# A fused block kernel on one core: the self attention's scores from one f32 matmul each to three matmuls in the rounded f32 form

## The reference, cut to what matters

```python
q = rms_norm(q, q_norm)          # (1, 1024, 8, 96), then rotary on the last 32
k = rms_norm(k, k_norm)
...
s = jnp.einsum('bqhd,bkhd->bhqk', qblk, k).astype(jnp.float32) * scale
p = jax.nn.softmax(s, axis=-1).astype(v.dtype)
return jnp.einsum('bhqk,bkhd->bqhd', p, v)
```

## Time and profile before

| | |
|---|---|
| median of 3 runs | 3533.15 us (3527.78 to 3535.71) |
| the profiled execution | 3533.38 us, span 3531.6 us, mean granted clock 0.944 |
| PE / PEld / DVE / ACT / POOL busy | 3136.1 / 2289.8 / 1394.0 / 905.2 / 149.6 us |
| `head_pairs` in the trace | 574.4 (first scores) to 826.8 us (last result stored) |

### The profile page before, as it was taken

The page is one execution under the profiler, slowest core; times in us unless marked ns, Lnnn a source line. Parts: engine busy times, 40 slices in busy tenths (PEclk is TensorE's granted clock), DMA queues, the critical chain, the costliest instruction groups (busy, mean ns, idle before and its releaser), DMA issues. The chain is left out here.

```text
span 3531.6 us, 35284 instructions
## 1 busy us (share of the span) xinstructions
PE 3136.1 (89%) x14324; PEld 2289.8 (65%) x14324; DVE 1394.0 (39%) x2157; ACT 905.2 (26%) x1452; POOL 149.6 (4%) x226
## 2 busy tenths in 40 slices
PE   7997777998898876887884998999999899999997
PEld 7786744446676663332332887888777688888886
DVE  3126846884444334111115647521215323333334
ACT  3432334443334210000004130021321232222221
POOL 0001011000000001111112000000000000000000
PEclk9998989999999997998996999999999899999999
DMA  3111000003220046999994131111112111111111
GB/s 96 48 46 4 10 13 1 1 1 113 72 84 7 30 194 244 420 421 419 413 399 196 36 75 64 51 48 48 33 57 96 36 48 48 48 48 50 52 48 72
DMA packets 140066, 370.01 MB, mean 105 GB/s; under 512 B 45888, under 2 KB 59840, under 8 KB 113920
## 3 DMA queue, kind: packets, MB, share of 16 engines
q1 hardware_dynamic: 129552, 346.97, 27.3%
q0 software_dynamic: 9216, 16.80, 1.3%
q10 hardware_dynamic: 1152, 4.19, 0.3%
HBM read 352.70 MB, written 32.83 MB: 109 GB/s over the span
## 5 line engine op out<-in xcount | busy, mean ns | idle before, releaser
L2546 PE MATMUL moe_ph<-moe_wgu,moe_rowsT 128*64 128x512 f32 x1024 | 265.4, 678 | 66.8 <-DMA moe_wgu<-in_moe_w_up_dram 37.7
L582 PE MATMUL mlp_ps<-mlp_high,mlp_w_cut 128*128 128x512 f32 x1024 | 317.3, 391 | 2.6 <-PEq L274 2.6
L582 PE MATMUL mlp_ps<-mlp_w_cut,mlp_hidden_high 128*128 128x512 f32 x1024 | 315.2, 389 | 0.0
L482 DVE TENSOR_TENSOR m_w_cut<-m_w_raw,m_w_cut 128x512 fp32r<-128x512 f32 (+1 forms) x86 | 80.8, 940 | 430.7 <-ACT m_w_cut L478 430.4
L482 DVE TENSOR_TENSOR mlp_w_cut<-mlp_w_raw,mlp_w_cut 128x1024 fp32r<-128x1024 f32 x63 | 77.2, 1225 | 397.0 <-ACT mlp_w_cut L478 396.6
L2546 PEld LDWEIGHTS moe_ph<-moe_wgu,moe_rowsT 128*64 128x64 f32 x1024 | 85.2, 155 | 226.7 <-issue 201.4
L582 PEld LDWEIGHTS mlp_ps<-mlp_high,mlp_w_cut 128*128 128x128 f32 x1024 | 193.5, 189 | 43.3 <-issue 3.0
L582 PEld LDWEIGHTS mlp_ps<-mlp_w_cut,mlp_hidden_high 128*128 128x128 f32 x1024 | 192.2, 188 | 39.9
L478 ACT ACTIVATE m_w_cut<-m_w_raw 128x512 fp32r<-128x512 f32 (+1 forms) x86 | 71.4, 831 | 515.3 <-PE m_gates_ps L582 192.8
L478 ACT ACTIVATE mlp_w_cut<-mlp_w_raw 128x1024 fp32r<-128x1024 f32 x63 | 66.7, 1058 | 526.1 <-PE mlp_ps L582 524.5
L582 PE MATMUL mlp_ps<-mlp_low,mlp_w_cut 128*128 128x512 f32 x512 | 200.1, 391 | 0.0
(11 more groups left out here) (534 smaller groups left out, 5850.4 us busy)
## 6 DMA issues: line engine op xcount, KB each, us to landing
moe_wgu<-in_moe_w_gate_dram SPq DMA_DIRECT2D x64, 1024.0 KB, 20.2
moe_wgu<-in_moe_w_up_dram SPq DMA_DIRECT2D x64, 1024.0 KB, 26.0
moe_wd<-in_moe_w_down_dram SPq DMA_DIRECT2D x64, 1024.0 KB, 20.1
mlp_w_raw<-in_w_ff_dram SPq DMA_DIRECT2D x64, 512.0 KB, 3.5
m_w_raw<-in_w_in_dram SPq DMA_DIRECT2D x48, 256.0 KB, 2.8
mix_w_raw<-in_w_in_dram SPq DMA_DIRECT2D x40, 256.0 KB, 2.6
m_w_raw<-in_w_in_dram SPq DMA_DIRECT2D x20, 512.0 KB, 3.8
x_w_raw<-in_x_w_kv_dram SPq DMA_DIRECT2D x16, 512.0 KB, 3.5
```

Of the source, the lines that this page charges most:

```text
L482: nc.vector.tensor_tensor(part(s, 1).bitcast(F32R), raw(s), part(s, 0), ALU.subtract).then_inc(low_ready, 1)
L582: ins = nc.tensor.matmul(ps[:, b, :r.shape[-1]], l, r, start=(k == 0 and sw is high and wh == 0), stop=(k == job.nk - 1 and sw is low))
L2546: ins = self.nc.tensor.matmul(self.ps_h[r, i].rearrange("p (i n) -> p i n", i=2), self.rowsT[:, i, k, r], self.wgu[:, w * self.parts + h, ...
```

## The change

The scores of a unit become six matmuls instead of two: for each half of the keys high x high, query high x key low, query low x key high, all in fp32r. The parts are made inside the unit loop. `make_highs(x)` is ACT's work, `make_lows(x)` DVE's; both are called at i = 4x + 1 and make the parts for chunk x + 1: a query part of 96x512 each time, and a key part of 96x1024 for the next new head where `due` names one. A call with x = -1 ahead of the loops makes chunk 0 and head 0. The lows are written in place over `qT` and `kT`; the query highs have a ring of two buffers, the key highs one of three. PE waits for both lows at the first unit of each chunk.

```diff
+        def due(x):
+            p, e = divmod(x, 4)
+            heads = [0] if x < 0 else [1] if x == 0 else [2 * p + 2] if e == 1 else [2 * p + 3] if e == 3 else []
+            return x + 1 if x + 1 < n // per else None, [h for h in heads if h < MH]
+
+        def make_highs(x):
+            q, heads = due(x)
+            if q is not None:
+                nc.scalar.activation(q_ring[:, q % 2].bitcast(F32R), qT[chunk(q)], ACT.Copy).then_inc(q_high_ready, 1)
+            for h in heads:
+                nc.scalar.activation(k_high(h).bitcast(F32R), kT[:, h], ACT.Copy).then_inc(k_high_ready, 1)
+
+        def make_lows(dve, x):
+            q, heads = due(x)
+            if q is not None:
+                dve.wait_ge(q_high_ready, q + 1)
+                nc.vector.tensor_tensor(q_low[chunk(q)].bitcast(F32R), qT[chunk(q)], q_ring[:, q % 2],
+                                        ALU.subtract).then_inc(q_low_ready, 1)
+            for h in heads:
+                dve.wait_ge(k_high_ready, h + 1)
+                nc.vector.tensor_tensor(k_low[:, h].bitcast(F32R), kT[:, h], k_high(h),
+                                        ALU.subtract).then_inc(k_low_ready, 1)
...
+                    if i % per == 0:
+                        pe.wait_ge(q_low_ready, i // per + 1)
+                        pe.wait_ge(k_low_ready, h + 1)
+                    q = [q_ring[:, i // per % 2, m % per * P:(m % per + 1) * P], q_low[:, h, m * P:(m + 1) * P]]
                     for s in range(nsb):
-                        ins = nc.tensor.matmul(ps_s[i % 2][:, s], qT[:, h, m * P:(m + 1) * P],
-                                               kT[:, h, s * CH:(s + 1) * CH], start=True, stop=True)
+                        k = [x[:, s * CH:(s + 1) * CH] for x in (k_high(h), k_low[:, h])]
+                        for x, y in ((0, 0), (0, 1), (1, 0)):
+                            ins = nc.tensor.matmul(ps_s[i % 2][:, s], q[x].bitcast(F32R), k[y].bitcast(F32R),
+                                                   start=(x == y), stop=(x == 1))
                     ins.then_inc(scored, 1)
...
+                make_lows(dve, -1)
                 for i in range(n + 2):
+                    if i % per == 1 and i < n:
+                        make_lows(dve, i // per)
                     if i >= 2:
                         copy_bank(dve, nc.vector.tensor_copy, i - 2, 1)
                     if 1 <= i <= n:
...
+                make_highs(-1)
                 for i in range(n + 1):
+                    if i % per == 1 and i < n:
+                        make_highs(i // per)
                     if i < n:
                         exps(i)
                     if i >= 1:
```

More of the change, by code:

```diff
@@ L790, in _, with head_pairs @@
                         copy_bank(act, lambda o, t: nc.scalar.activation(o, t, ACT.Copy), i - 1, 0)
-def head_pairs(c, name, qT, kT, v, room, mixT, rq):
+def head_pairs(c, name, qT, kT, k_two, lows, v, room, mixT, rq):
     nc = c.nc
@@ L820, in head_pairs, with chunk @@
         copied = [c.sem(f"{name}_copied{s}") for s in range(nsb)]
+        q_low, k_low = lows
+        k_third = sbuf(ctx, nc, f"{name}_k_high_third", [QK, T])
+        q_ring = sbuf(ctx, nc, f"{name}_q_high", [QK, 2, CH])
+        q_high_ready, q_low_ready, k_high_ready, k_low_ready = [c.sem(f"{name}_{x}") for x in (
+            "q_high_ready", "q_low_ready", "k_high_ready", "k_low_ready")]
+        k_high = lambda h: k_two[:, h % 3] if h % 3 < 2 else k_third[:]
+        def chunk(x):
+            p, e = divmod(x, 4)
+            return (slice(None), 2 * p + e % 2, slice(e // 2 * CH, (e // 2 + 1) * CH))
+        def due(x):
+            p, e = divmod(x, 4)
+            heads = [0] if x < 0 else [1] if x == 0 else [2 * p + 2] if e == 1 else [2 * p + 3] if e == 3 else []
[16 more added lines that the diff above has]
+                                        ALU.subtract).then_inc(k_low_ready, 1)
         def copy_bank(eng, copy, i, s):
@@ L1664, in mix_first @@
         s = lambda n, shape, dt=F32: sbuf(own, nc, n, shape, dt)
+        first_home = nc.sbuf_base
         mla_in = s("mla_in", [P, NT, QR + KVR + ROPE])
@@ L1746, in mix_first @@
                         x[:].rearrange("p m d -> p (m d)"), qT[:], kT[:], v[:], rq[:])
-        head_pairs(c, "mla_attn", qT, kT, v,
+        k_high = nc.alloc_sbuf_tensor_at("mla_k_high", [QK, 2, T], F32, offset=first_home)
+        lows = [lies(f"mla_{n}_low", [QK, MH, T], kb) for n, kb in (("q", 0), ("k", 32))]
+        head_pairs(c, "mla_attn", qT, kT, k_high, lows, v,
                    x[:].rearrange("p m d -> p (m d)").rearrange("p (j e q) -> p j e q", e=2, q=CH), hT, rq)
```

## The result

The changed kernel takes 3589.66 us (3588.39 to 3594.41, 3 runs), before 3533.15: a ratio of 1.0164, interval 1.0147 to 1.0181, or 56.5 us more. The forecast was 3585.

The account below looks back on a forecast made before the run. The prediction took the DVE and ACT chain (3.697 us a unit) and PE's round (3.751) as nearly equal bounds. Faster scores -2.2, stalls +39.4, start +5.7, clock +8.4 gave +51.3 us on 3533.4, so 3585 us; own range 3574 to 3597.

Parts of the forecast that it names:

- What bounds the kernel: Attention loop: DVE and ACT pace 3.697 us, PE's round 3.751; faster scores gain only 40 x 0.054 = 2.2 us.
- the chain: DVE and ACT in a unit: maximum, bias, exponentials, sum, reciprocal, scaling, next maximum; 3.697 us with nothing of PE in it.
- The stall: DVE waits for ACT's highs at i = 4x + 1: +2.17 us 8 times, +3.67 with key part 6 times, +39.4 us.
- The start: Attention stage's start: first maximum +3.8 us, call at i = 1 +2.6, unit 2 -0.7; sum +5.7 us.
- The clock: PE's clock falls to half at the 14 later stalls, delaying a maximum by 0.6 us each: +8.4 us.
- the first rival: PE's clock holds in the short stalls; only the six with a key part pay, 3.6 us: 3580 us, chance 0.14.
- two bounds: Delay of a maximum behind a pause of PE: 0 if the clock is back, 1.18 us if transposes and scores run at half.
- The sum: Whole kernel: -2.2 + 39.4 + 5.7 + 8.4 = +51.3 us on 3533.4 us, giving 3585 us.
- The faster rival: PE sets the attention loop's pace; a unit falls from 3.75 to 3.41 us: 3518 us, chance 0.05.
- the place that I had named: The maximum's start on DVE, 0.67 us after the scaling; it decides whether units can be packed tighter than 3.70 us.
- my signs: Profile after: L850 idle near 2.4 us, L854 some 0.4, maxima 3.70, 5.9 or 7.4 apart, stage 43 to 51 us longer.
- the rival in which the clock stays down longer: PE's clock falls at each stall and PE paces one or two units, 14 x 1.86 = 26 us: 3603 us, chance 0.13.

Follow-up runs that it names:

- fast scores alone: Six fp32r matmuls in every unit, parts made only once ahead of the loop, against the kernel before: 3530.02 us, ratio 0.9994.
- the chain apart: Changed kernel with a third probabilities buffer, PE transposing unit i - 2 and DVE taking the next maximum before the scaling: 3518.21 us, 0.9964 of the kernel before.
- the lows later: Changed kernel with DVE making the lows one unit later, at i = 4x + 2: 3539.51 us, 1.0022 of the kernel before.
- the highs earlier: Changed kernel with ACT making the highs one unit earlier, at i = 4x: 3544.62 us, 1.0033 of the kernel before.
- PE kept busy: Changed kernel with 10 or 18 extra fp32r matmuls on PE in each pause behind a make_lows call: 3578.94 us, 1.0138 of the kernel before.
- the splits alone: Changed kernel with highs and lows made but not read, scores the two f32 matmuls of before: 3585.70 us, 1.0153 of the kernel before.

## Why the prediction was right, point by point

- **What bounds the kernel.** Two paces, 3.697 for the chain and 3.751 for PE, and a gain of 2.2 us for faster scores. Shown: fast scores alone run at the chain's pace and change nothing; with the chain apart, PE's 0.3 us a unit appear. PE's full matmul share was no promise of a gain.
- **The stall.** Predicted steps from the maximum: low at 3.80, key low at 4.76, copy 5.90, reciprocal 6.50, maximum 7.37. Measured: 3.83, 4.77, 5.92, 6.52, 7.37. The sum of the 14 calls was 39.4 and is 39.6. That the wait and not the work costs is shown from both sides, by the lows later and the highs earlier.
- **The start.** 3.8 + 2.6 - 0.7 = 5.7 was forecast; 3.9 + 2.6 - 1.4 = 5.1 came. Unit 2 was earlier than I had it: the clock came back at 596.7, in the middle of its scores, which I had taken at half throughout.
- **The clock.** The term that was mis-sized: 0.6 us a pause, 8.4, where 11.5 came, 0.82 a pause. It fell in or just behind all 14 pauses, short ones too, so the first rival, which held it up there, is out, and with it the rule of the Trainium skill (TensorE: Matmul & The Clock Gate, HAM oscillation) as it would apply here: a query-only pause leaves PE without a record for some 2 us (from unit 17 on) and the clock drops. I had reckoned with one late maximum behind a pause; behind most of the long ones two came, 1.01 and then up to 0.70. The 0.6 was the middle of two bounds and stands for no pause: the six long ones cost 1.44 us each, over my upper bound of 1.18, and the eight short ones 0.36. That the mean came near was in part luck.
- **The sum.** 51.3 us was forecast. The account of the trace has 54.0: 0.2 more for the calls, 0.6 less for the start, 3.1 more for the clock. The medians have 56.5.
- **The rest.** The order of DVE and ACT, not the amount of work, made 49 of the 56.5 us. It did not set the sign: with the lows later the kernel is still some 8 us slower than before (1.0012 to 1.0032), and only the order two behind makes it faster. The faster rival failed on the place that I had named: the chain was not packed tighter. Of my signs, L854 waited 0.26 us and not 0.4, the stage grew by 54.9 us (261.1 to 316.0) where I had 43 to 51, and the pace within a chunk is 3.70 only where the clock is up; PE kept busy shows that the late maxima are the clock's. Two figures don't come out of their terms: the rival in which the clock stays down longer sums to 3602 us, and the upper end of the forecast's own range to 3596. Nothing hangs on either.

## What to carry to other kernels

When a pipeline's engines run hand-written loops, a job made "ahead" is only ahead if both its halves are: look where in its own order each engine meets the wait, and move the consumer one step behind the producer. Before making the busiest engine faster, divide the time between equal events by their count: if two loops stand close to each other (here 1.5% apart), the gain ends at the second, and it's the recurrence that must be cut first.

## What was not expected of the hardware

- The granted clock fell to half behind each of 14 pauses of PE (1.95 to 4.9 us without a matmul record), while in the kernel with fast scores alone it stayed at full over more than 200 us with pauses of 0.2 or 1.2 us in nearly every unit. With the splits alone it fell behind six of 14 pauses only, and one of 3.40 us passed at full clock. Filling the pauses with useless matmuls (216 of them) kept it at full and made the kernel faster, by 10.7 us from unit 0 to 63 in the traces and some 9 in the runs.
- `mla_prepare`, the same in all kernels, took 101 to 110 us in ten traces, and the longer it took, the longer its clock was at half: 31 us in the two shortest (101.0 and 102.5 us), 48 in the two longest (109.5 us). Such a stage adds several microseconds of scatter to runs that compare others.
